# Token sums of the FFN down products on VectorE ahead of the projection, and one odd weight split with them

## The reference, cut to what matters

```python
D_MODEL = 1024
SEQ = 256
D_FF = 2816

def swiglu(x, w_gate, w_up, w_down):
    return (jax.nn.silu(x @ w_gate) * (x @ w_up)) @ w_down

def first_block(x, ...):
    x = x + 0.5 * swiglu(rmsnorm(x, ffn1_norm[l]), ffn1_w_gate[l], ffn1_w_up[l], ffn1_w_down[l])
    ...
    x = x + 0.5 * swiglu(rmsnorm(x, ffn2_norm[l]), ffn2_w_gate[l], ffn2_w_up[l], ffn2_w_down[l])
    return rmsnorm(x, final_norm)

def second_block(x, mem, ...):
    h = h + FFN_RES_WEIGHT * swiglu_2(rmsnorm_2(h, ffn1_norm[i]), ffn1_w_gate_up[i], ffn1_w_down[i])
    ...
    h = h + FFN_RES_WEIGHT * swiglu_2(rmsnorm_2(h, ffn2_norm[i]), ffn2_w_gate_up[i], ffn2_w_down[i])
    return rmsnorm_2(h, final_norm)
```

## Time and profile before

| what | value |
|---|---|
| median of three runs | 1369.29 us |
| the profiled execution | 1374.1 us, of it 1372.3 us span |
| TensorE busy (PE) | 1333.9 us, 97% |
| weight loads (PEld) | 1121.8 us, 82% |
| VectorE busy | 783.2 us, 57% |
| ScalarE busy | 791.6 us, 58% |
| GpSimd busy | 643.2 us, 47% |
| mean granted TensorE clock | 0.994 |
| DMA queue of SyncE's loads | 230.89 MB, 49.0% |
| DMA queue of GpSimd's transfers | 16.78 MB, 6.3% |
| one load of 1 MB, issue to landing | 5.0 us (median) |
| one adding transfer of 1 MB | 9.8 us (median) |

### The profile page before, as it was taken

How to read it: one execution, slowest core, us unless ns; L and a number is a source line. 1 busy time by engine, 2 the same in 40 slices (tenths; PEclk the granted TensorE clock), 3 DMA queues, 4 the chain that set the end, 5 groups by cost and what they waited for, 6 DMA issues and landing times.

```text
span 1372.3 us, 18846 instructions
## 1 busy us (share of the span) xinstructions
PE 1333.9 (97%) x7312; PEld 1121.8 (82%) x7312; DVE 783.2 (57%) x1026; ACT 791.6 (58%) x1083; POOL 643.2 (47%) x240
## 2 busy tenths in 40 slices
PE   9999899999999999999899999999999999999987
PEld 8888777888888778888678887788888888888876
DVE  6655556955555475555466559754335632555555
ACT  7655347456555556556447687667434654655543
POOL 1449533474546755448643331035525524444952
PEclk9999999999999999999999999999999999999999
DMA  9664964224655586554884646345854544555392
...
DMA packets 41113, 256.90 MB, mean 187 GB/s; under 512 B 6192, under 2 KB 6736, under 8 KB 12112
## 3 DMA queue, kind: packets, MB, share of 16 engines
q1 hardware_dynamic: 36832, 230.89, 49.0%
q0 software_dynamic: 2304, 16.78, 6.3%
...
## 4 chain that ended last, share of the span: by engine, by line
PE 52%; issue 21%; POOL 16%; DMA 5%; ACT 3%; DVE 3%; POOLq 0%; SPq 0%; ACTq 0%; DVEq 0%
PE acc L353 13%; PE acc L355 12%; PE acc L354 12%; POOL wlo L334 10%; DMA raw<-in_t_ffn_down 4%; POOL forms L994 2%; POOL form_lo L1010 2%; ACT whi L329 2%; PE acc L2790 2%; DVE wlo L334 2%; POOL forms L999 1%; PE acc L368 1%; PE work L1141 1%; PE acc L2791 1%; PE work L434 1%
## 5 line engine op out<-in xcount | busy, mean ns | idle before, releaser
L334 POOL TENSOR_TENSOR wlo<-raw,whi 128x2048 fp32r<-128x2048 f32 (+1 forms) x112 | 499.8, 4484 | 496.9 <-ACT whi L329 488.3
L329 ACT ACTIVATE whi<-raw 128x2048 fp32r<-128x2048 f32 (+1 forms) x237 | 437.5, 1857 | 132.6 <-DMA raw<-in_t_ffn_down 78.4
L334 DVE TENSOR_TENSOR wlo<-raw,whi 128x2048 fp32r<-128x2048 f32 x125 | 334.8, 2678 | 225.7 <-ACT whi L329 225.4
L368 PE MATMUL acc<-xT,whi 128*128 128x512 f32 x1208 | 427.8, 396 | 0.0
L369 PE MATMUL acc<-xT,wlo 128*128 128x256 f32 x1384 | 373.7, 280 | 0.0
L368 PEld LDWEIGHTS acc<-xT,whi 128*128 128x128 f32 x1208 | 226.5, 188 | 50.5 <-DVE xT L473 1.1
L369 PEld LDWEIGHTS acc<-xT,wlo 128*128 128x128 f32 x1384 | 261.3, 189 | 7.3
L353 PE MATMUL acc<-whi,xT 128*128 128x512 f32 x416 | 168.3, 405 | 0.0
L355 PE MATMUL acc<-whi,xT 128*128 128x512 f32 x416 | 162.5, 391 | 0.0
L354 PE MATMUL acc<-wlo,xT 128*128 128x512 f32 x416 | 162.3, 390 | 0.0
L831 DVE TENSOR_TENSOR work<-acc,low_parts 128x512 f32<-128x512 f32 x88 | 61.5, 699 | 104.9 <-ACT low_parts L713 102.1
...
## 6 DMA issues: line engine op xcount, KB each, us to landing
...
```

What stands on the lines that cost most here:

```text
L329: act.activation(granule(whi, u, i), granule(raw, u, i), ACT.Copy).then_inc(hi_ready, 1)
L334: eng.tensor_tensor(granule(wlo, u, i), granule(raw, u, i), granule(whi, u, i).bitcast(F32), ALU.subtract).then_inc(lo_odd if g % 2 else l ...
L368: pe.matmul(to, hi[:, c], both_parts(kt), start=first, stop=False)
```

## The change

It has four parts, all in the four feed-forward parts:

- The forms are made by VectorE, between the loop and step 9, and `form_lo` by VectorE after step 9. GpSimd makes neither.
- ScalarE waits for the forms and rounds them ahead of its step 9, not after it.
- lo of granule 9 of the down projection is made by VectorE, right after that of 8. The two semaphores of the lo counts are now named by engine, and `lo_signal` counts which granules belong to which.
- In the down projection VectorE adds P4 into x ahead of lo of granule 4 (before: after it), and the second add of P1 ahead of lo of granule 12.

```diff
     units = plan_stream()
+    GRANULES_BY_VECTOR = (9,)
+    of_down = {units[f"ffn{f}.down0"].g + n for f in range(4) for n in GRANULES_BY_VECTOR}
...
+    def lo_signal(g):
+        by_vector = [n for n in range(g + 1) if n % 2 == 0 or n in of_down]
+        if g in by_vector:
+            return lo_by_vector, len(by_vector) + FIRST_LO[0]
+        return lo_by_gpsimd, g + 1 - len(by_vector) + FIRST_LO[1]
...
@@ ffn_scalar
-        step(9)
-
-        down = [units[f"ffn{f}.down{j}"] for j in range(len(DOWN) // 2)]
         act.wait_ge(forms_made, 3 * f + 1)
         act.activation(form_hi[:, :, :], forms[:, :, :], ACT.Copy).then_inc(forms_rounded, 1)
+        step(9)
+
+        down = [units[f"ffn{f}.down{j}"] for j in range(len(DOWN) // 2)]
...
@@ ffn_vector
+        def block_of(i, j):
+            return forms[:, 4 * j:4 * j + 4, i * P:(i + 1) * P]
+
+        def form(to, other, op):
+            dlink(dve.tensor_tensor(block_of(*to), block_of(*to), block_of(*other), op))
+            dwait(dve)
+
+        dve.wait_ge(hidlo_done, PIECES * f + 8)
+        if b == B_FFN2:
+            dve.wait_ge(x_rescaled, NT)
+        dlink(dve.tensor_tensor(forms[:, :, :], hid_hi[:, 0:KD, :].bitcast(F32), hid_lo[:, 0:KD, :].bitcast(F32), ALU.add))
+        dwait(dve)
+        form((1, 1), (1, 0), ALU.subtract)
+        form((1, 0), (0, 0), ALU.add)
+        form((0, 0), (1, 1), ALU.subtract)
+        form((0, 1), (0, 0), ALU.subtract)
+        dve.sem_inc(forms_made, 1)
         step(9)
+        dve.wait_ge(forms_rounded, f + 1)
+        for j in range(2):
+            kts = slice(4 * j, 4 * j + 4)
+            dve.tensor_tensor(form_lo[j][:, :, :], forms[:, kts, :], form_hi[:, kts, :].bitcast(F32),
+                              ALU.subtract).then_inc(forms_made, 1)
...
-        split_lo(dve, down[2], 0)
...
         add_to_x(0, 0, PRODUCT_BANK["P4"], MINUS_HALF_RSTD)
         add_to_x(0, 1, PRODUCT_BANK["P4"], HALF_RSTD)
-        split_lo(dve, down[3], 0)
+        lo(4)
+        lo(6)
...
-        split_lo(dve, down[4], 0)
+        lo(8)
+        lo(9)
...
@@ ffn_pool
-        pool.wait_ge(hidlo_done, PIECES * f + 8)
-        if b == B_FFN2:
-            pool.wait_ge(x_rescaled, NT)
-        link(pool, pool.tensor_tensor(forms[:, :, :], hid_hi[:, 0:KD, :].bitcast(F32), hid_lo[:, 0:KD, :].bitcast(F32),
-                                      ALU.add))
-        form((1, 1), (1, 0), ALU.subtract)
-        form((1, 0), (0, 0), ALU.add)
-        form((0, 0), (1, 1), ALU.subtract)
-        form((0, 1), (0, 0), ALU.subtract)
-        pool.sem_inc(forms_made, 1)
         step(9)
-        for j in range(2):
-            pool.wait_ge(forms_rounded, f + 1)
-            kts = slice(4 * j, 4 * j + 4)
-            pool.tensor_tensor(form_lo[j][:, :, :], forms[:, kts, :], form_hi[:, kts, :].bitcast(F32),
-                               ALU.subtract).then_inc(forms_made, 1)
-        split_lo(pool, down[0], 1)
+        lo(1)
         add_to_slot(4)
-        split_lo(pool, down[1], 1)
+        lo(3)
         add_to_slot(6)
         add_to_slot(8)
-        split_lo(pool, down[2], 1)
-        split_lo(pool, down[3], 1)
+        lo(5)
+        lo(7)
         add_to_slot(12)
-        for j in (4, 5, 6, 7):
-            split_lo(pool, down[j], 1)
+        lo(11)
+        lo(13)
+        lo(15)
```

More of the change, by code:

```diff
@@ L236, in build @@
     hi_ready = sem("hi_ready")
-    lo_even, lo_odd = sem("lo_even"), sem("lo_odd")
+    lo_by_vector, lo_by_gpsimd = sem("lo_by_vector"), sem("lo_by_gpsimd")
     gran_done = sem("gran_done")
@@ L263, in wait @@
         eng.wait_ge(s, value if it is None else it * per + value)
+    def lo_signal(g):
[3 more added lines that the diff above has]
+        return lo_by_gpsimd, g + 1 - len(by_vector) + FIRST_LO[1]
     def wait_lo(eng, g, it=None):
-        wait(eng, lo_odd if g % 2 else lo_even, g // 2 + 1 + FIRST_LO[g % 2], it, RING // 2)
+        signal, count = lo_signal(g)
+        wait(eng, signal, count, it, RING // 2)
     def wait_unit_done(eng, u, it=None):
@@ L386, in multiply_first @@
                     pe.matmul(to, hi[:, j, c], both_parts(kt), start=kt == 0, stop=False)
-            pe.wait_ge(lo_odd if i else lo_even, j + 1)
+            pe.wait_ge(lo_by_gpsimd if i else lo_by_vector, j + 1)
             for m in range(2):
@@ L396, in multiply_first @@
                 ready(kt)
-                pe.wait_ge(lo_odd, kt - 3)
+                pe.wait_ge(lo_by_gpsimd, kt - 3)
                 mm = row_block(pe, ffn_pair(m), WIDE_COLS[m], kt, hi[:, kt - 4, :], lo[:, kt - 4, :], False, kt == KD - 1)
@@ L786, in ffn_scalar @@
             step(4, it)
+        act.wait_ge(forms_made, 3 * f + 1)
+        act.activation(form_hi[:, :, :], forms[:, :, :], ACT.Copy).then_inc(forms_rounded, 1)
         step(9)
         down = [units[f"ffn{f}.down{j}"] for j in range(len(DOWN) // 2)]
-        act.wait_ge(forms_made, 3 * f + 1)
-        act.activation(form_hi[:, :, :], forms[:, :, :], ACT.Copy).then_inc(forms_rounded, 1)
         low(19)
@@ L878, in ffn_vector @@
             join(0)
-            split_lo_first(dve, 2, (2, 3), (hi_ready, KD + 2), lo_even)
+            split_lo_first(dve, 2, (2, 3), (hi_ready, KD + 2), lo_by_vector)
             join(1)
@@ L920, in add_to_x, with lo @@
                 last_added[t, half] = signal, value
-        step(10, None, lambda: split_lo(dve, down[0], 0))
-        step(11, None, lambda: split_lo(dve, down[1], 0))
-        split_lo(dve, down[2], 0)
+        def lo(n):
+            split_lo(dve, down[n // 2], n % 2)
+        step(10, None, lambda: lo(0))
+        step(11, None, lambda: lo(2))
         if b + 1 == B_MIX2:
@@ L938, in ffn_vector @@
         add_to_x(1, 1, PRODUCT_BANK["P7"], MINUS_HALF_RSTD, products_added, 2 * f + 1)
-        split_lo(dve, down[5], 0)
+        lo(10)
         dve.wait_ge(gran_done, down_done(f, 8))
@@ L943, in ffn_vector @@
         add_to_x(0, 0, PRODUCT_BANK["P1"], HALF_RSTD, resid_done, 2 * b + 1)
+        add_to_x(1, 1, PRODUCT_BANK["P1"], MINUS_HALF_RSTD)
         if b + 1 == B_FFN2:
             apply_final1(dve, 0)
-        split_lo(dve, down[6], 0)
-        add_to_x(1, 1, PRODUCT_BANK["P1"], MINUS_HALF_RSTD)
+        lo(12)
         dve.wait_ge(gran_done, down_done(f, 9))
@@ L950, in ffn_vector @@
         add_to_x(1, 1, PRODUCT_BANK["P2"], MINUS_HALF_RSTD)
-        split_lo(dve, down[7], 0)
+        lo(14)
         if b == B_FFN0:
@@ L988, in add_to_slot, with lo @@
                            accum_op=ALU.add).then_inc(added_to_slot[g % RING], 16)
-        def block_of(i, j):
-            return forms[:, 4 * j:4 * j + 4, i * P:(i + 1) * P]
-        def form(to, other, op):
-            link(pool, pool.tensor_tensor(block_of(*to), block_of(*to), block_of(*other), op))
-        pool.wait_ge(hidlo_done, PIECES * f + 8)
-        if b == B_FFN2:
-            pool.wait_ge(x_rescaled, NT)
-        link(pool, pool.tensor_tensor(forms[:, :, :], hid_hi[:, 0:KD, :].bitcast(F32), hid_lo[:, 0:KD, :].bitcast(F32),
-                                      ALU.add))
-        form((1, 1), (1, 0), ALU.subtract)
-        form((1, 0), (0, 0), ALU.add)
-        form((0, 0), (1, 1), ALU.subtract)
-        form((0, 1), (0, 0), ALU.subtract)
-        pool.sem_inc(forms_made, 1)
-        step(9)
-        for j in range(2):
-            pool.wait_ge(forms_rounded, f + 1)
-            kts = slice(4 * j, 4 * j + 4)
-            pool.tensor_tensor(form_lo[j][:, :, :], forms[:, kts, :], form_hi[:, kts, :].bitcast(F32),
-                               ALU.subtract).then_inc(forms_made, 1)
-        split_lo(pool, down[0], 1)
+        step(9)
+        def lo(n):
+            split_lo(pool, down[n // 2], n % 2)
+        lo(1)
         add_to_slot(4)
-        split_lo(pool, down[1], 1)
+        lo(3)
         add_to_slot(6)
         add_to_slot(8)
-        split_lo(pool, down[2], 1)
-        split_lo(pool, down[3], 1)
+        lo(5)
+        lo(7)
         add_to_slot(12)
-        for j in (4, 5, 6, 7):
-            split_lo(pool, down[j], 1)
+        lo(11)
+        lo(13)
+        lo(15)
         for u in next_units:
```

4 lines of the change are left out of this document (2 added, 2 removed).

## The result

The changed kernel took 1358.05 us (median of six runs, 1353.97 to 1359.87), the kernel before beside it 1369.53 (1364.58 to 1372.77): ratio 0.9916, 95% interval 0.9894 to 0.9939. That is 11.5 us faster where the forecast had 15.6, and 4 us above the forecast of 1354, inside the range of 1343 to 1365. A later set of six gave 1359.31 against 1367.2, 0.9935 (0.991 to 0.996): 8 us.

A forecast was written before the change was run, and what follows sets the result against it. TensorE, busy 97% of the span, bounds the kernel, with 29.2 us of waits in the down projections. 4 x 3.5 = 14.0 us plus 3.2 less 1.6 of slow clock gain 15.6: 1354 us, range 1343 to 1365.

The forecast's parts named there:

- Sums 5.3 us, from 107.1 to 112.4.: Between the loop and step 9: VectorE's five sum operations take 5.3 us, 2.4 of them hidden in its idle time.
- New wait of 1.3 before piece 19.: TensorE in each stage: piece 19 waits 1.3 us for join(17), as form_hi now stands ahead of low(17) on ScalarE.
- lo(1) ends at 133.75.: GpSimd, down projection, first stage: lo(1) waits for ScalarE and ends at 133.75 against 135.02, 1.27 us earlier.
- Granules 1 and 4 without a wait, granule 5 at 154.7 after a wait of 3.0.: TensorE, down projection: waits before 1 (1.22 us) and 4 (1.03) go; granule 5 begins at 154.7, waiting 3.0 us.
- The adding transfer takes 10.77 us again: Down projection, granule 4: from GpSimd's issue of the adding transfer to hi(4) takes 10.77 us, as before.
- rival 3: Much faster: granule 4's adding transfer shrinks by 2.2 us, gaining 8.8 more over four stages; 1343 us, chance 0.12.
- lo(6) 2.3 us.: VectorE, down projection: lo(6) gets in before GpSimd and takes near 2.3 us instead of 6.43.
- The race at lo(10): VectorE's lo(10) against GpSimd's lo(11): granule 10 starts 4.3 us earlier if VectorE is first, 2.7 if GpSimd is.
- It lies 4.8 above the median of 1369.29, and the median becomes 1353.7.: Whole kernel: the profiled 1374.1 us less 15.6 gives 1358.5; taken 4.8 above the median, this makes the median 1353.7.
- four terms of 3.5: Four down projections: each starts granule 10 3.5 us earlier, the middle of 4.3 and 2.7; 14.0 us in sum.
- Rival 1: Waits only move: data for granules 9, 10 and 11 land at most 1.3 us earlier; gain 5, 1364 us, chance 0.15.
- Rival 2: Slower: VectorE's sums take GpSimd's 12.0 us, granule 10 starts 2.4 us later in each stage; 1379 us, chance 0.05.

The follow-up runs named there:

- again: The changed kernel, no edit, profiled a second time: median 1359.31 us, profiled execution 1361.25 us.
- before_2: The kernel before the change, no edit, profiled a second time: 1366.86 us.
- before_3: The kernel before the change, no edit, profiled a third time: 1364.38 us.
- after_3: The changed kernel, no edit, profiled a third time: 1355.73 us.

## Why the prediction was right, and what in it was wrong

- **Sums 5.3 us, from 107.1 to 112.4.** 107.11 to 112.29, 5.2. Right.
- **New wait of 1.3 before piece 19.** 1.0 in each part. TensorE went on at 115.57, within 0.1 us of the forecast, but had come to the piece at 114.58, 0.2 later than before.
- **lo(1) ends at 133.75.** 133.62, and it waits for ScalarE as said (5.59 us). The working is loose by 0.1 us in two places (step 9 is 9.2 us and then 9.1; 129.05 + 4.65 is 133.70), which changes nothing.
- **Granules 1 and 4 without a wait, granule 5 at 154.7 after a wait of 3.0.** The first two are gone (0.4 is left before 4 in one part); granule 5 at 154.57 after 2.83. Right.
- **The adding transfer takes 10.77 us again (against rival 3).** 10.87, though lo(2) started only at 135.16, after the issue was over. Rival 3 fell: a VectorE split beside the issue was not what the transfer lost.
- **lo(6) 2.3 us.** 2.29 in the first part. The Trainium skill (SBUF — State Buffer, "SBUF: two separate sides") has the two engines exclude each other; the traces agree: lo(10) in the second part took 4.25 us in `again`, where GpSimd began 0.28 us earlier, and 2.29 in the first profile, where VectorE was first.
- **The race at lo(10): granule 10 4.3 us earlier if won, 2.7 if lost.** Won in the first part: 171.04, forecast 171.3. But lo(10) began at 167.37 and lo(11) at 168.37, some 0.9 and 1.7 us later than forecast, so the path to the race was off by more than its margin, as the prediction had feared. The last down product of each part ends the count: 199.56, 524.91, 717.47 and 1366.25 in the profile before, 193.61, 514.59, 702.16 and 1346.10 in the first after (four won), 193.14, 518.04, 709.50 and 1353.40 in `again` (parts 2 and 3 lost). Part by part the first gained 6.0, 4.4, 5.0 and 4.8 us, of which some 1.6 and 3.1 in parts 1 and 2 are stretches at half clock that went; `again` gained 6.4, 0.5, 1.1 and 4.9. Both cases exist, as said. Not foreseen was that each of these two lost races has the lower clock behind it, some 1.6 us each.
- **"It lies 4.8 above the median of 1369.29, and the median becomes 1353.7."** This is the step that was off, by 4.3 us, and by 5.6 in the second set. I took 15.6 us off the median as if the typical execution had the waits of the profiled one. For a profiled execution like the first the sum did well: with four races won its upper end was 20.4 us, and the first changed profile, the fastest of its six, is 20.1 under 1374.1. But 1374.1 is at the top of the kernel's scatter, with three waits before granule 10, 8.2 us, and each of the four terms of 3.5 counts from such a wait (or, in the second part, from 6.8 us at half clock). `before_2` has one such wait, `before_3` none, and where they are absent there is less to give back. The slowest profiles of the two kernels are 12.9 us apart (1374.1 and 1361.25), the fastest 10.4 (1364.38 and 1353.97), `before_3` and `after_3` 8.7. The last difference adds up from its rows: waits in the down projections and at piece 19 go from 21.0 to 14.9 us, 6.1, and two stretches of 3.4 us at half clock fewer give 3.2 at the prediction's price, together 9.3. That the median came within 4 us owes something to the middle value taken for the race (3.5) and to the stretch left in.
- **Rival 1** (1364, waits only move) was not the case: lo(6) and lo(10) got their pace. **Rival 2** did not come, as the sums took 5.2 us; its slope is shown: 2 us per part for 2.3 us of sums.

Still open is why a fall of the clock follows one wait of 2.8 us and not the next. In the three executions of the kernel before it followed one, three and four of the four waits before granule 5, in those of the changed kernel one, one and two. Not tried: front adds ahead of lo(10), and the wait for lo(10) in the kernel before.
